# Expert loop of a float32 encoder on one Trainium2 core: the gate/up product taken ahead of the lo piece, the result copy moved into the next expert, the Silu table outside the loop, and the last expert written into both branches

## What is computed

```python
def moe_swiglu(h, router_w, wg, wu, wd):
    logits = jnp.einsum('bsd,de->bse', h, router_w)
    top_v, top_i = lax.top_k(logits, TOP_K)           # 2 of 8
    top_p = jax.nn.softmax(top_v, axis=-1)
    gates = ...                                        # one hot of top_i, times top_p
    out = jnp.zeros_like(h)
    for e in range(N_EXPERTS):                         # wg, wu: 1024 x 3584, wd: 3584 x 1024
        out = out + gates[..., e:e + 1] * swiglu(h, wg[e], wu[e], wd[e])
    return out
```

## Time and profile before

| what | value |
|---|---|
| median of 3 runs | 1426.88 us (1424.85 to 1426.97) |
| the profiled execution's own time | 1427.06 us |
| its span, first to last instruction | 1425.3 us |
| mean granted TensorE clock | 0.986 |
| PE, DVE, ACT busy | 96%, 82%, 71% of the span |
| experts 1 to 7 (loop) | 407.1 to 1256.7 us, one every 120.70 us |
| eighth expert and end | 1256.7 to 1425.3 us |

### The profile page before, as it was taken

One profiled execution on the slowest core, in us unless ns is written; L12 is line 12 of the kernel. 1 busy time (PEld: TensorE's weight loads), 2 busy tenths in 40 slices (PEclk: granted clock), 3 DMA queues, 4 the chain that ended last, 5 costly groups with the idle time before them and its releaser, 6 DMA issues.

```text
span 1425.3 us, 19188 instructions
## 1 busy us (share of the span) xinstructions
PE 1363.0 (96%) x6780; PEld 1146.2 (80%) x6780; DVE 1161.8 (82%) x1244; ACT 1005.7 (71%) x1166; POOL 64.1 (4%) x63
## 2 busy tenths in 40 slices
PE   5999999999879999999999999999999999989997
PEld 5866999998668888887887888888788888868876
DVE  4776655556679989998998998999899899979984
ACT  4545644445557878788788787878888787768874
POOL 1230000000040000000000000000000000000000
PEclk9999999999989999999999999999999999999999
DMA  8401954357359999989989998998999999999920
GB/s 319 178 0 32 392 209 151 119 207 266 133 180 368 353 335 395 394 323 395 395 325 392 396 396 321 397 394 321 395 393 360 357 395 394 396 336 383 363 102 30
DMA packets 175585, 427.24 MB, mean 300 GB/s; under 512 B 3760, under 2 KB 8496, under 8 KB 175408
## 3 DMA queue, kind: packets, MB, share of 16 engines
q1 hardware_dynamic: 171072, 412.10, 77.5%
q0 software_dynamic: 3024, 11.01, 2.0%
q10 hardware_dynamic: 1440, 3.48, 0.7%
HBM read 420.28 MB, written 6.29 MB: 299 GB/s over the span
## 4 chain that ended last, share of the span: by engine, by line
PE 88%; DVE 6%; ACT 3%; issue 1%; DMA 1%; ACTq 0%; SPq 0%; DVEq 0%
PE G L1209 17%; PE G L1211 17%; PE G L1210 17%; PE Y L1209 10%; PE Y L1211 10%; PE Y L1210 10%; PE G L1505 2%; DVE lo_ring L702 1%; DVE ring L764 1%; ACT hi_ring L421 1%; DMA ring<-in_w_in 1%; PE G L1303 1%; PE Y L1323 1%; DVE xT_lo L732 1%; PE G L1427 0%
## 5 line engine op out<-in xcount | busy, mean ns | idle before, releaser
L702 DVE TENSOR_TENSOR lo_ring<-ring,hi_ring 128x1024 fp32r<-128x1024 f32 x692 | 837.4, 1224 | 173.5 <-ACT hi_ring L421 131.3
L421 ACT ACTIVATE hi_ring<-ring 128x1024 fp32r<-128x1024 f32 x692 | 731.2, 1061 | 274.8 <-PE G L1211 163.4
L1209 PE MATMUL G<-hi_ring,xT_hi 128*128 128x512 f32 x896 | 356.1, 397 | 10.9 <-DVE lo_ring L702 5.8
L1211 PE MATMUL G<-lo_ring,xT_hi 128*128 128x512 f32 x896 | 350.9, 392 | 0.0
L1210 PE MATMUL G<-hi_ring,xT_lo 128*128 128x512 f32 x896 | 350.3, 391 | 0.0
L1209 PE MATMUL Y<-hi_ring,mT_hi 128*128 128x512 f32 x568 | 223.9, 394 | 0.0
L1211 PE MATMUL Y<-lo_ring,mT_hi 128*128 128x512 f32 x568 | 221.3, 390 | 0.0
L1210 PE MATMUL Y<-hi_ring,mT_lo 128*128 128x512 f32 x568 | 221.1, 389 | 0.0
L1209 PEld LDWEIGHTS G<-hi_ring,xT_hi 128*128 128x128 f32 x896 | 169.1, 189 | 47.7 <-DVE lo_ring L702 8.8
L1211 PEld LDWEIGHTS G<-lo_ring,xT_hi 128*128 128x128 f32 x896 | 169.1, 189 | 36.3
L1210 PEld LDWEIGHTS G<-hi_ring,xT_lo 128*128 128x128 f32 x896 | 169.4, 189 | 33.8
(11 more groups left out here) (227 smaller groups left out, 988.4 us busy)
## 6 DMA issues: line engine op xcount, KB each, us to landing
ring<-in_moe_wg SPq DMA_DIRECT2D x56, 2048.0 KB, 10.6
ring<-in_moe_wu SPq DMA_DIRECT2D x56, 2048.0 KB, 11.7
ring<-in_moe_wd SPq DMA_DIRECT2D x56, 2048.0 KB, 11.7
ring<-in_ffn_wg SPq DMA_DIRECT2D x5, 2048.0 KB, 7.9
ring<-in_ffn_wu SPq DMA_DIRECT2D x5, 2048.0 KB, 10.1
ring<-in_ffn_wd SPq DMA_DIRECT2D x5, 2048.0 KB, 8.3
ring<-in_ple_gate_w SPq DMA_DIRECT2D x4, 2048.0 KB, 7.9
ring<-in_w_in SPq DMA_DIRECT2D x3, 2048.0 KB, 17.4
```

Source lines behind the costliest of these rows:

```text
L421: act.activation(hi_ring[:, n % AHEAD, :], where, ACT.Copy).then_inc(hi_done, 1)
L702: dve.tensor_tensor(lo_ring[:, n % AHEAD, :], where, hi_ring[:, n % AHEAD, :].bitcast(F32), ALU.subtract).then_inc(lo_done, 1)
L1209: pe.matmul(dst, s_hi, m_hi, start=start, stop=False, skip_group_check=True)
L1211: return pe.matmul(dst, s_hi, m_lo, start=False, stop=stop, skip_group_check=True)
```

## The change

- **Product first.** In DVE's step behind the fourth wu piece, the wait for `pe_piece` and `xsilu` and the multiplication come ahead of the wait for `hi_done` and the low piece, in the loop and in the last expert.
- **Result copy later.** `y_copy` is taken out of ACT's step 83 and put behind the high piece of step 2 of the next expert. `y_copy(it)` copies what the expert before left in `Y`. In the first round there is none, and the copy (of whatever `Y` holds) goes to a block of its own. `y_rows` has one block more, the row bases move by one block, PE's waits for `y_out` and POOL's for `y_rows_in` count one more. The copy of the seventh result now stands in step 2 of the last expert, and `last_head` ends with a wait for it.
- **Silu outside.** The Silu of one value stands once, ahead of the loop.
- **Register loads.** `value_load` of `most` stands ahead of the loop on ACT, DVE, PE and POOL (there ahead of the store of block 0).
- **Branch.** The condition is turned (`n_most <= P`), the case that runs comes first, and the code of the last expert up to the end is compiled into both branches on ACT, DVE and PE (on POOL `pairs`). On SP only the condition and the order are turned; its last loads still stand behind both.

```diff
-        with sp.If(n_most > P):
+        with sp.If(n_most <= P):
+            last_head(MAIN)
+        with sp.Else():
             expert_loads(MAIN, ITERS, MAIN)
             last_head(ITERS)
-        with sp.Else():
-            last_head(MAIN)
...
+        def y_copy(it):
+
+            act.wait_ge(y_rows_in, it * 16 + 16)
+            act.activation(y_sb, Y[:, 0:2, :].rearrange("p b n -> p (b n)"), ACT.Copy).then_inc(y_out, 1)
+
         def experts(first, last, extra):
             with act.Fori(first, last) as it:
-                act.activation(unused[:, 0:1], eps[:, 0:1], ACT.Silu)
                 for q in range(XP):
...
-                    if q == XP - 1:
-                        act.wait_ge(y_rows_in, it * 16 + 16)
-                        act.activation(y_sb, Y[:, 0:2, :].rearrange("p b n -> p (b n)"), ACT.Copy).then_inc(y_out, 1)
                     hi(PB + n, None, None, ring[:, XSLOT[c], (n % 4) * PIECE:(n % 4 + 1) * PIECE])
+                    if q == 2:
+                        y_copy(it)
...
+        act.wait_ge(tabs_done, 1)
+        n_most = act.value_load(most[0:1, 0:1])
         act.activation(unused[:, 0:1], eps[:, 0:1], ACT.Silu)
...
+        experts(0, MAIN, 0)
+        with act.If(n_most <= P):
+            last_expert(MAIN)
+        with act.Else():
+            for half in range(2):
+                gathered_hi(half, 2 * NE + 1 + half)
+            experts(MAIN, ITERS, 1)
+            last_expert(ITERS)
...
+                    if name == "moe_wu" and s == 3:
+                        dve.wait_ge(pe_piece, it * XP + (PB + q + 1))
+                        dve.wait_ge(xsilu, it * GROUPS + (j + 1))
+                        dve.tensor_tensor(x_act, x_act, G[:, 1, :], ALU.mult).then_inc(xmul, 1)
                     dve.wait_ge(hi_done, it * XP + (PB + n + 1))
                     lo(PB + n, ring[:, XSLOT[c], (n % 4) * PIECE:(n % 4 + 1) * PIECE])
...
+        n_most = pool.value_load(most[0:1, 0:1])
+        store(0)
         experts(0, MAIN, 0)
-        n_most = pool.value_load(most[0:1, 0:1])
-        with pool.If(n_most > P):
+        with pool.If(n_most <= P):
+            pairs(MAIN, MAIN + 1)
+        with pool.Else():
             gather(NE)
             experts(MAIN, ITERS, 1)
-            store(ITERS, ITERS + 1)
-            pool.wait_ge(gath_mm, 2 * (ITERS + 2))
-            pairs(ITERS + 1)
...
-            pe.wait_ge(y_out, done + 1)
-
+            pe.wait_ge(y_out, done + 2)
...
+        n_most = pe.value_load(most[0:1, 0:1])
         experts(0, MAIN, 0)
-        n_most = pe.value_load(most[0:1, 0:1])
-        with pe.If(n_most > P):
+        with pe.If(n_most <= P):
+            last_head(MAIN, MAIN + 1)
+            last_expert()
+        with pe.Else():
             pe.wait_ge(xlo_done, 2 * NE)
             token_list(NE + 1)
             gather(16 * NE)
             experts(MAIN, ITERS, 1)
             last_head(ITERS, ITERS + 2)
-        with pe.Else():
-            last_head(MAIN, MAIN + 1)
```

More of the change, by code:

```diff
@@ L631, in experts @@
                         gathered_hi(s - 1, it * 2 + (3 + 2 * extra + s - 1))
[L633 to L641, removed]
         def last(q):
@@ L651, in last @@
             act.activation(hi_ring[:, q % AHEAD, :], ring[:, LSLOT[i], off:off + PIECE], ACT.Copy).then_inc(last_hi, 1)
-        act.activation(unused[:, 0:1], eps[:, 0:1], ACT.Silu)
[L654 to L686, removed]
-            act.activation(tok[:, b // 2, (b % 2) * 512:(b % 2 + 1) * 512], Y[:, b, :], ACT.Sigmoid,
-                           scale=rstd[:, 5, b // 2:b // 2 + 1]).then_inc(sig_gate, 1)
+        def last_expert(done):
+            for q in range(XP):
+                name, j, _ = LAST[last_chunk(q)]
+                s = q % 4
+                if q == XP - 1:
+                    for c in range(2):
+                        act.wait_ge(last_piece, XP)
+                        act.activation(y_hi[c], Y[:, c, :].rearrange("p (k n) -> p k n", k=4), ACT.Copy).then_inc(yhi_done, 1)
+                last(q + AHEAD)
+                if q == 2:
+                    y_copy(done)
+                if name == "moe_wg" and s == 3:
+                    if j >= 1:
+                        act.wait_ge(last_at_mm, j)
+                        act.activation(aT_hi[:, (j - 1) % 2, :, :], G[:, 2, :].rearrange("p (f n) -> p f n", f=4),
+                                       ACT.Copy).then_inc(last_at_hi, 1)
+                    act.activation(x_act, G[:, 0, :], ACT.Silu).then_inc(last_silu, 1)
+                if name == "moe_wu" and s == 3 and j == 3:
+                    act.wait_ge(sp_mm, 1)
+                    act.activation(spread[:, :], Y[:, 3, 0:SEQ], ACT.Copy).then_inc(sp_out, 1)
+                if name == "moe_wd" and s == 0 and j == GROUPS - 2:
+                    act.wait_ge(last_at_mm, GROUPS)
+                    act.activation(aT_hi[:, (GROUPS - 1) % 2, :, :], G[:, 2, :].rearrange("p (f n) -> p f n", f=4),
+                                   ACT.Copy).then_inc(last_at_hi, 1)
+            last(XP + AHEAD)
+            norm(5)
+            norm_hi(5, Y8)
+            for q in range(XP + AHEAD + 1, LPIECE[NL]):
+                last(q)
+            act.activation(unused[:, 1:2], eps[:, 0:1], ACT.Sigmoid)
+            act.wait_ge(rstd_done, T * 6)
+            for b in range(2 * T):
+                if b < 2 * T - 1:
+                    act.wait_ge(bank_done, 3 * 3 + b + 1)
+                else:
+                    act.wait_ge(last_piece, LPIECE[NL])
+                act.activation(tok[:, b // 2, (b % 2) * 512:(b % 2 + 1) * 512], Y[:, b, :], ACT.Sigmoid,
+                               scale=rstd[:, 5, b // 2:b // 2 + 1]).then_inc(sig_gate, 1)
@@ L1057, in experts @@
                         gathered_lo(s - 2, it * 2 + (3 + 2 * extra + s - 2))
-        experts(0, MAIN, 0)
-        dve.wait_ge(tabs_done, 1)
-        n_most = dve.value_load(most[0:1, 0:1])
[L1062 to L1069, removed]
         def last(q):
@@ L1130, in _ @@
+        dve.wait_ge(tabs_done, 1)
+        n_most = dve.value_load(most[0:1, 0:1])
+        experts(0, MAIN, 0)
+        links = chain[0]
+        with dve.If(n_most <= P):
+            last_expert()
+        with dve.Else():
+            chain[0] = links
+            picks(slice(NE, NE + 1), pick_done)
+            token_list(NE)
+            for half in range(2):
+                gathered_lo(half, 2 * NE + 1 + half)
+            experts(MAIN, ITERS, 1)
+            last_expert()
     @block.gpsimd
```

237 lines of the change are left out of this document (118 added, 119 removed).

## The result

The changed kernel took 1411.53 us (median of 4 runs, 1411.04 to 1413.63), the kernel before beside it 1426.93 (4 runs, 1424.85 to 1428.25). The ratio is 0.9901, 95% interval 0.9882 to 0.992: faster by 15.4 us. The profiled execution took 1411.34 us, 1409.5 of it span.

The account below looks back on a forecast made before the run. PE, busy 96% of the span, was taken as bound by its own work, leaving only a few stands. Gains of 19.7 us less costs of 6.9 gave net 12.8: 1414.1 us, range 1409.5 to 1420.5.

Parts of the forecast that it names:

- Product first, in the rounds: Last transposes of seven rounds: the product fits into DVE's wait for the high piece, PE's distance shrinks; gain 6.4 us.
- Product first, in the eighth expert: Last transposes of the eighth expert: PE's distance falls from 2.03 to 0.23 us; gain 1.8 us.
- Turn: Six turns between rounds: without result copy and table load on ACT, PE's stall of 0.69 us goes; gain 4.1 us.
- Loop's end: Behind the loop: no taken branch, so PE's 5.41 us stand shrinks to 0.23 and the slow stretch goes; gain 7.4 us.
- Register load on DVE: Loop's start: the load stands directly ahead of the low piece that ends PE's 3.26 us wait; cost 0.5 us.
- First round: Near 422 us: moved copy waits for block 0's store to land; stall 3.3 plus slow stretch 1.7, cost 5.0 us.
- End: Kernel's end: engines jump over the other branch side, mostly covered; cost 0.4 us, bounds 0 and 2.4.
- the stand behind the loop stays: Rival, loop's end: code isn't there in time even without a taken branch, 7.4 us not gained; 1420.5 us, chance 0.09.
- the back end places table loads anew in the loop: Rival, loop body: loads at the first copy and ahead of Silu, the second exceeding ACT's air; 1417.6 us, chance 0.08.
- too little air behind the copy: Rival, each round on ACT: 0.6 us lost per round and the turn's gain eaten; 1418 us, chance 0.04.
- low pieces held back by the product: Rival, every group on DVE: product first delays low pieces, 19 us over 56 groups; 1433 us, chance 0.03.
- the first round costs its upper bound: Rival, first round and end at their upper bounds: 3.4 + 2.0 us more; 1419.5 us, chance 0.14.

Follow-up runs that it names:

- e1: The kernel before with only DVE's product put ahead of the low piece, in the loop and the last expert; 1416.69 us, ratio 0.9923.
- e2: The kernel before with only the Silu of one value moved ahead of the loop, result copy left in place; 1421.37 us, ratio 0.9951.
- e5: The changed kernel with the Silu of one value back in the loop body, result copy staying in step 2; 1411.28 us, ratio 0.9908.
- e8: The kernel before with only register loads ahead of the loop, the condition turned and the last expert in both branches; 1420.70 us, ratio 0.9971.
- e4: As e3, but the last expert compiled once, behind the two branches, with the condition turned; 1412.20 us, ratio 0.9893 to the kernel before.
- e3: The changed kernel with the result copy, its store order and waits back at their old place; 1408.89 us, ratio 0.9875 to the kernel before.
- e7: As e3, with DVE's row-number chain moved from the loop's start into steps 0 to 2 of the last expert; 1405.20 us, ratio 0.9869.
- e9: The changed kernel (copy moved) with DVE's row-number chain moved into the last expert as in e7; 1414.26 us, ratio 0.9923 to the kernel before.
- e6: The changed kernel with POOL's register load behind the store of block 0 and DVE's ahead of its table wait; 1411.96 us, ratio 0.9922.
- e10: The kernel of e7 run once more, in one series with e9; 1404.25 us, ratio 0.9852 to the kernel before.

## Why the prediction was right

The forecast was 1414.1 us within 1409.5 to 1420.5; it came to 1411.5. The three gains are where it put them. The amounts below are by the starts of the same matmul. By its own steps:

- **Product first, in the rounds: right in size, its reason incomplete.** 6.4 us forecast, 6.7 measured, and e1 shows that it comes from this edit alone. But the step said that DVE could take the product up as soon as the fourth wu piece ends. DVE of the changed kernel, where that piece's last matmul starts at 761.45:

```profile
758.95 3.88 DVE L709 TENSOR_TENSOR lo_ring<-ring,hi_ring 128x1024 fp32r<-128x1024 f32 x3
762.75 0.68 DVE L1046 TENSOR_TENSOR misc<-misc,G 128x512 f32<-128x512 f32 x1
```

  DVE still has a low piece in hand and comes to the product 1.3 us after that start. In the rounds the token transposes on PE, about 1 us, cover it.
- **Product first, in the eighth expert: over-sized.** 1.8 us forecast, 1.4 measured. The step took the product as ended before PE comes. With no token transposes in between, the low piece that DVE finishes first shows as the 0.68 us at 1358.72.
- **Turn: right in size, wrong in its cause.** 4.1 forecast, 4.4 measured. The step gave the gain to "without both". e2 and e5 show that either alone gives all of it, so the size was right because PE's stall caps it, whatever the cause: PE had 0.59 us to win, and each of the two ACT pieces is over 1 us long. Of the "next two" starts at 0.33 only one is at that distance; the 0.10 in the sum is right.
- **Loop's end: right.** 7.4 forecast (5.2 and 2.2), 7.5 measured (5.2 and 2.3), and e8 shows it alone. The Trainium skill's sentence that a taken branch out of the fetched window has to wait for a fetch (Runtime: NRT & Kernel Launch, Instruction fetch mechanics) agrees with e4: not taken 71 ns, taken 5.1 us, in one kernel. That the time is a fetch no trace shows, and being taken isn't enough: PE's branch back to the loop's start, taken six times in the changed kernel, took 208 to 253 ns.
- **Wait for the copy in the eighth expert:** 1.0 forecast, 1.0 measured, and 1.0 between e3 and the changed kernel.
- **Register load on DVE: under-sized.** 0.5 forecast from a load of 549 ns. It took 846 ns here, and the stand grew by 0.8.
- **First round: the stand a little over-sized, the slow stretch wrong.** Forecast 3.3 and 1.7, measured 2.6 and 0.2. The store was issued at 419.95, 0.95 later than forecast, but landed in 2.9 us instead of 3.4, and PE came 1 us later too. The slow stretch was taken over from the stand before it by its length alone, and that isn't what decides. These 1.5 us and the 0.7 of the stand are the larger part of what the forecast was too high by. The 3.4 us of landing were a choice between two rows of 3.4 and 6.5; the argument for the lower one, that the weight loads come later too, fits the 2.9 here against the 8 of e7. (With a landing at 425.5 the upper bound is 8.1, not 8.4.)
- **End:** 0.4 forecast; DVE's jump took 2.9 us and stayed hidden, with 0.4 to spare. The +0.4 between the last matmul and the end isn't the jump's: SP's drain comes last, behind the last store of the output, which landed 2.4 us after its issue instead of 2.0.
- **The rest** is the final stage's slow stretch, 1.6 us in the profile of the kernel before and none in the changed kernel's, which no step of the change touches, and the 0.8 us ahead of the loop the other way.

Three of the signs it named did not come: DVE's product began 1.3 us after the last start of the fourth wu piece instead of within 0.8, the distance in the eighth expert stayed at 0.68 instead of under 0.35, and the clock was not down behind the second stand.

Of the rivals, that the stand behind the loop stays is out by e8 and the 71 ns. That the back end places table loads anew in the loop is out too. The last two groups of ACT's table loads in the changed kernel, by line:

```profile
L687 ACT ACT_TABLE_LOAD x1 | 1.3, 1283 | 0.0
L675 ACT ACT_TABLE_LOAD x1 | 1.3, 1283 | 0.0
```

L687 is the one ahead of the loop, L675 one of the final stage, and no line of the loop has one. The Trainium skill's rule that loads are placed per block (ScalarE activation tables, Table sets in the compiler and the runtime) did not bring one here. A load at the start of the loop body costs nothing (e5). The rival had its 3.5 us from a load behind the copy, a place that no run tests.

The two rivals that hold PE back in every round, too little air behind the copy and low pieces held back by the product, are out by the round of 119.04 us.

The rival that the first round costs its upper bound had the right place, but not the reason. In e9 the moved copy takes 10 us there with a landing of 2.9: what grew is PE's lead, not the landing. In the changed kernel it cost little because the stand before it had already made PE late.

What stays open: why the same stand is followed by slow starts in one execution and not in the next, and why a jump over the other side costs microseconds and the loop's own branch doesn't.

## What to carry to other kernels

Before moving two things away from a stall, price each alone. Here either the table load or the copy could stay, and moving the copy brought a new wait on a store's landing at the loop's entry, which grows by each microsecond that PE gains ahead of it. When a stall has a slow operation of DVE ahead of it, look at what POOL runs at that time: small operations that nobody needs yet can cost 3.9 us at one place and next to nothing at another. For an `If` whose outcome is known to be the same nearly always, let that side follow directly and carry the code behind it, so that the jump falls at the end, where something else is still on its way. Count the jump on every engine: in e4 ACT's alone would have held PE nearly as long as PE's own.

## What the runs showed of the hardware

- Small DVE operations beside POOL's large ones took 1.61 and 2.31 us and ended within 0.1 us of POOL's (changed kernel), against 0.17 and 0.22 us with POOL idle (e7). Between low pieces and POOL's sums the engines took turns: a low piece took 3.42 us instead of 1.22 and a sum 3.39 instead of 2.39 (e7).
- A jump over the side that doesn't run cost PE 5.1 (e4), 6.2 (e1) and 6.6 us under full weight traffic, 3.3 (e8) and 3.4 us (changed kernel) at the end. Not taken 71 ns. The branch back to the loop's start, taken six times, cost PE 208 to 253 ns and ACT 45 to 68 (changed kernel).
- A register load took 490 ns on PE and 495 on POOL (changed kernel), 549 and 846 (changed kernel) on DVE.
- One and the same store landed 2.9 us after its issue where PE stood (changed kernel, e6, e9), 3.3 in e3 and 8.1 where PE and the weight loads ran on (e7).
- Slow starts (0.43 us apart) behind a stand do not follow from its length: none behind 2.8 us (changed kernel, 423) and 3.5 us (e4), seven behind 3.5 us in the final stage of the kernel before, none in the changed kernel's and some thirteen in e3's, about ten behind 7.9 us (e9). Each is worth 0.2 us. e7 and e10 are one kernel, and their profiled executions differ through this by 1.3 us in the final stage and by 0.7 near 24 us.
